# Block-diagonal 128x128 products in the chunk inverse of a gated DeltaNet, with a new order of the scan stage

## What is computed

```python
m_low = where(strict, einsum('cd,ed->ce', k * beta, k) * decay, 0)
t_inv = solve(eye + m_low, eye)          # lower triangular, 64x64
u = t_inv @ (v * beta);  w = t_inv @ (k * beta * exp(g))
a_intra = (q @ k.T) * decay
# scan over the 16 chunks
v_new = u - w @ state
o = (q * exp(g)) @ state + a_intra @ v_new
state = state * exp(g_last) + (k * exp(g_last - g)).T @ v_new
```

## Time and profile before

| | |
|---|---|
| median of three runs | 1391.61 us |
| profiled execution, its own time | 1390.32 us |
| its span | 1388.5 us |
| PE busy | 1371.7 us (99%) |
| DVE, ACT, POOL busy | 1027.0, 606.9, 177.9 us |
| instructions | 21991 |

### The profile page before, as it was taken

One profiled execution on the slowest core, in us unless ns is written; L12 is line 12 of the kernel. 1 busy time (PEld: TensorE's weight loads), 2 busy tenths in 40 slices (PEclk: granted clock), 3 DMA queues, 4 the chain that ended last, 5 costly groups with the idle time before them and its releaser, 6 DMA issues.

```text
span 1388.5 us, 21991 instructions
## 1 busy us (share of the span) xinstructions
PE 1371.7 (99%) x8400; PEld 1139.1 (82%) x8400; DVE 1027.0 (74%) x1890; ACT 606.9 (44%) x1306; POOL 177.9 (13%) x163
## 2 busy tenths in 40 slices
PE   9999999999999999999999999999999999999997
PEld 8788888787888888788888888888888888888885
DVE  6999976866888887645268796666665777777778
ACT  4655534422444443532113545545555544444540
POOL 4322332230000000236700000000000000000002
PEclk9999999999999999999999999999999999999998
DMA  6233245766344531245612153344435875555423
GB/s 216 91 113 115 111 163 182 243 221 179 94 107 117 135 103 51 77 166 177 239 55 91 69 189 130 143 167 167 167 133 212 295 239 181 165 159 178 128 69 121
DMA packets 123496, 206.83 MB, mean 149 GB/s; under 512 B 40864, under 2 KB 61568, under 8 KB 121088
## 3 DMA queue, kind: packets, MB, share of 16 engines
q1 hardware_dynamic: 113312, 183.93, 39.8%
q10 hardware_dynamic: 10080, 21.50, 4.1%
HBM read 142.92 MB, written 62.47 MB: 148 GB/s over the span
## 4 chain that ended last, share of the span: by engine, by line
PE 88%; DVE 6%; DMA 3%; SPq 2%; issue 1%; ACT 0%; POOL 0%; ACTq 0%; DVEq 0%; POOLq 0%
PE ps L2223 7%; PE ps L2603 6%; PE ps L2604 6%; PE ps L2602 6%; PE ps L2587 6%; PE ps L2585 6%; PE ps L2586 6%; PE ps L2171 5%; PE ps L2173 5%; PE ps L2172 5%; PE ps L2289 4%; PE ps L2109 4%; PE ps L2111 4%; PE ps L2110 4%; PE ps L2479 2%; PE ps L2483 2%
## 5 line engine op out<-in xcount | busy, mean ns | idle before, releaser
L2602 PE MATMUL ps<-thi,shi 128*128 128x512 f32 x416 | 161.8, 389 | 0.0
L2603 PE MATMUL ps<-tlow,shi 128*128 128x512 f32 x416 | 161.8, 389 | 0.0
L2604 PE MATMUL ps<-thi,slow 128*128 128x512 f32 x416 | 161.8, 389 | 0.0
L947 ACT ACTIVATE thi<-b 128x512 fp32r<-128x512 f32 x104 | 65.5, 630 | 111.8 <-PE ps L2604 111.2
L1993 DVE TENSOR_TENSOR tlow<-b,thi 128x512 fp32r<-128x512 f32 x104 | 71.8, 690 | 52.8 <-ACT thi L947 52.7
L937 POOL TENSOR_TENSOR zt<-zt,ln2gb 128x256 f32<-128x256 f32 x4 | 3.4, 852 | 691.5 <-ACT zt L1403 691.5
L2602 PEld LDWEIGHTS ps<-thi,shi 128*128 128x128 f32 x416 | 78.1, 188 | 16.4
L2603 PEld LDWEIGHTS ps<-tlow,shi 128*128 128x128 f32 x416 | 78.1, 188 | 16.2
L2604 PEld LDWEIGHTS ps<-thi,slow 128*128 128x128 f32 x416 | 78.1, 188 | 16.1
L1986 DVE TENSOR_TENSOR slow<-sraw,shi 128x512 fp32r<-128x512 f32 x104 | 71.4, 686 | 21.6 <-ACT shi L947 20.9
L947 ACT ACTIVATE shi<-sraw 128x512 fp32r<-128x512 f32 x104 | 65.0, 625 | 28.9 <-DMA zt<-xpark 16.3
(11 more groups left out here) (445 smaller groups left out, 3827.2 us busy)
## 6 DMA issues: line engine op xcount, KB each, us to landing
raw<-in_wblk SPq DMA_DIRECT2D x55, 512.0 KB, 4.1
sraw<-hpark SPq DMA_DIRECT2D x104, 256.0 KB, 2.7
hpark<-hq SPq DMA_DIRECT2D x16, 1024.0 KB, 4.9
b<-in_wblk SPq DMA_DIRECT2D x64, 256.0 KB, 3.6
wraw<-in_wblk SPq DMA_DIRECT2D x30, 512.0 KB, 3.8
hpark<-hq SPq DMA_DIRECT2D x16, 768.0 KB, 4.9
park<-cb ACTq DMA_DIRECT2D x34, 256.0 KB, 3.3
park<-cacc ACTq DMA_DIRECT2D x12, 512.0 KB, 3.2
```

The costliest lines, as they stand in the source:

```text
L947: cp = lambda o_, i_: act.activation(o_, i_, ACT.Copy)
L2602: mm(outp, shi[s][:, ts], thi[m][:, :], start=first, stop=False, skip_group_check=True)
L2603: mm(outp, shi[s][:, ts], tlow[m][:, :], start=False, stop=False, skip_group_check=True)
L2604: return mm(outp, slow[s][:, ts], thi[m][:, :], start=False, stop=final, skip_group_check=True)
```

## The change

mm_ (128x256) becomes mmd (128 x 4 heads x 128), which DVE writes in two halves, each chunk's 64x64 block on the diagonal of its head's 128x128; the rest is zero. a_y then issues one product for each head, 128x128 weights by 64 moving columns, in place of two 64x64 ones. DVE's a_r of level 5 no longer writes rinv, but the two diagonal blocks of a new rind, and waits for the products b_vn of the tile before, which read it. b_vn takes rind's 128x128 as weights and all 128 rows of xs, with 128 moving columns as before. Three memsets set the zeros once. a_u, a_ut and a_t1 keep their blocks. The lists of PE, DVE and ACT in a step get another order, FILLS gets 31 gaps in place of 28 and other numbers (384 in all, as before), and SP's load_ks moves ahead of load_dec. load_pair is written out in place, with the same instructions. The diff, cut to its core:

```diff
--- before.py
+++ after.py
 N_STEP, N_LAST = 7 * NP, 8
 N_STD = 3
 FILLS = [
-    [1, 0, 0, 4, 0, 0, 0, 0, 0, 11, 0, 5, 1, 0, 1, 0, 4, 0, 1, 0, 1, 0, 0, 5, 6, 1, 2, 0],
-    [0, 3, 5, 0, 6, 1, 1, 0, 0, 3, 0, 2, 2, 3, 0, 3, 0, 0, 0, 0, 0, 0, 1, 0, 0, 1, 8, 2],
-    [0, 0, 0, 0, 0, 3, 2, 2, 1, 0, 0, 0, 0, 0, 0, 0, 4, 0, 0, 13, 0, 0, 1, 0, 0, 9, 0, 0],
-    [0, 0, 0, 0, 0, 3, 2, 2, 1, 0, 0, 0, 0, 0, 0, 0, 4, 4, 0, 9, 0, 0, 2, 0, 4, 4, 0, 0],
-    [0, 0, 0, 0, 0, 2, 0, 4, 2, 0, 0, 0, 0, 0, 0, 0, 4, 5, 0, 8, 0, 1, 2, 0, 2, 5, 0, 0],
-    [0, 0, 0, 0, 0, 3, 2, 2, 1, 0, 0, 0, 0, 0, 0, 0, 4, 5, 0, 8, 0, 1, 2, 0, 0, 7, 0, 0],
-    [0, 0, 0, 0, 0, 3, 2, 2, 1, 0, 0, 0, 0, 0, 0, 0, 4, 5, 0, 8, 0, 0, 1, 0, 4, 5, 0, 0],
-    [0, 0, 0, 0, 0, 3, 2, 2, 1, 0, 0, 0, 0, 0, 0, 0, 4, 0, 0, 13, 0, 0, 1, 0, 4, 5, 0, 0],
-    [0, 0, 0, 0, 0, 2, 4, 0, 2, 0, 0, 0, 0, 0, 0, 0, 0, 0, 0, 19, 1, 3, 0, 0, 0, 2, 0, 0],
-    [0, 0, 0, 3, 0, 4, 0, 8, 2, 1, 2, 0, 0, 0, 0, 1, 0, 19, 0, 0, 0, 0, 7, 0, 0, 4, 0, 6],
+    [2, 5, 0, 0, 0, 0, 0, 0, 5, 4, 0, 0, 1, 5, 2, 0, 0, 0, 3, 0, 1, 0, 0, 0, 2, 7, 0, 3, 0, 2, 1],
+    [5, 0, 7, 0, 0, 3, 0, 3, 0, 0, 3, 2, 1, 0, 3, 0, 0, 3, 0, 0, 0, 0, 1, 0, 0, 3, 2, 0, 0, 0, 8],
+    [0, 2, 0, 0, 0, 4, 1, 1, 0, 0, 0, 1, 0, 0, 0, 1, 1, 6, 0, 3, 1, 1, 0, 0, 0, 4, 1, 0, 3, 0, 0],
+    [2, 2, 0, 1, 0, 5, 0, 0, 0, 1, 0, 2, 0, 0, 0, 0, 0, 5, 0, 2, 5, 0, 1, 0, 0, 4, 1, 0, 7, 0, 0],
+    [0, 0, 0, 1, 0, 5, 0, 1, 0, 0, 0, 2, 0, 0, 0, 0, 1, 9, 0, 1, 0, 2, 0, 0, 0, 4, 2, 0, 6, 0, 0],
+    [0, 0, 0, 1, 0, 5, 0, 1, 0, 0, 0, 2, 0, 0, 0, 0, 1, 4, 0, 2, 3, 0, 1, 0, 0, 5, 1, 0, 2, 0, 0],
+    [3, 2, 0, 1, 0, 4, 1, 1, 0, 0, 0, 2, 0, 0, 0, 0, 0, 10, 0, 1, 0, 0, 1, 0, 0, 5, 0, 0, 5, 0, 0],
+    [2, 0, 0, 1, 0, 4, 1, 1, 0, 0, 0, 2, 0, 0, 0, 1, 1, 8, 0, 1, 2, 0, 0, 0, 0, 5, 0, 0, 3, 0, 0],
+    [1, 3, 0, 1, 0, 3, 2, 0, 0, 0, 2, 0, 0, 0, 0, 0, 0, 6, 0, 6, 1, 0, 2, 1, 0, 5, 0, 1, 1, 0, 0],
+    [0, 3, 0, 2, 1, 1, 6, 0, 0, 7, 1, 3, 0, 0, 0, 2, 0, 9, 3, 0, 7, 0, 0, 3, 6, 0, 0, 0, 4, 0, 6],
 ]
...
+        rind = workb("rind", 512, [P, NH, P])
+        mmd = at("mmd", 96, [P, NH, P], extra=26496)
-        mm_, ml, *tb = [worka(name, 256, [P, NH, CH]) for name in ("mm", "ml", "tb0", "tb1")]
+        ml, *tb = [worka(name, 256, [P, NH, CH]) for name in ("ml", "tb0", "tb1")]
...
                     load_dv(t + 2)
+                load_ks(t + 1, (t + 1) % 2)
                 if t < NT - 2:
                     load_dec(t + 2)
                 load_qk(t + 1)
-                load_ks(t + 1, (t + 1) % 2)
...
                 if t is not None: b_vn(t, 0)
+                if s in BEHIND: split_hi(BEHIND[s])
                 if a is not None: a_t1(a, q)
+                if a is not None: a_eg(a)
                 if t is not None: b_exps(t, 0)
+                if t is not None: b_vn(t, 1)
+                if t is not None: b_osq(t)
                 if t is not None: b_pt(t, 0)
-                if a is not None: a_eg(a)
-                if t is not None: b_vn(t, 1)
-                if s in BEHIND: split_hi(BEHIND[s])
+                if first < last: late_half(first)
                 if t is not None: b_ya(t, 0)
-                if t is not None: b_osq(t)
-                if first < last: late_half(first)
+                if n is not None: a_scalars(n, p)
+                if n is not None: a_squares_k(n)
                 if t is not None: b_exps(t, 1)
-                if n is not None: a_scalars(n, p)
                 if n is not None: a_squares_q(n)
-                if n is not None: a_squares_k(n)
                 if t is not None: b_pt(t, 1)
+                if t is not None: b_ya(t, 1)
                 if first + 1 < last: late_half(first + 1)
                 if first + 2 < last: late_half(first + 2)
-                if t is not None: b_ya(t, 1)
...
+                dve.memset(mmd[:, :, :], 0.0)
+                dve.memset(rind[:, :, :], 0.0)
+                dve.memset(xs[CH:P, :, :], 0.0)
...
                 tt(ml[:, :, :], half(A0, 0), em0[:, :, :], ALU.mult).then_inc(m_ok, 1)
-                tt(mm_[:, :, :], half(A0, 0), eml[:, :, :], ALU.mult).then_inc(m_ok, 1)
+                for r in chunks:
+                    ins = tt(mmd[r, :, r], half(A0, 0)[r], eml[r, :, :], ALU.mult)
+                ins.then_inc(m_ok, 1)
                 dve.wait_ge(m_ok, 2 * t + 1)
                 tt(tb[0][:, :, :], bh(msk(M_ID)), ml[:, :, :], ALU.subtract).then_inc(t1_ok, 1)
 
                 dve.wait_ge(u_mm, 5 * t + l)
                 if l == 1:
                     dve.wait_ge(r0_ok, t + 1)
-                tt(rinv[p][:, :, :], rinv[p][:, :, :], half(A1, 0), ALU.subtract).then_inc(r_ok if l < 5 else a_done, 1)
+                if l < 5:
+                    tt(rinv[p][:, :, :], rinv[p][:, :, :], half(A1, 0), ALU.subtract).then_inc(r_ok, 1)
+                else:
+                    if t:
+                        dve.wait_ge(vn_mm, 2 * t)
+                    for r in chunks:
+                        ins = tt(rind[r, :, r], rinv[p][r, :, :], half(A1, 0)[r], ALU.subtract)
+                    ins.then_inc(a_done, 1)
...
                 if t is not None: b_max(t, 0, p)
+                if t is not None: b_state(t, 0, p)
                 if a is not None: a_att(a, q)
                 if s == -1: clear()
-                if t is not None: b_state(t, 0, p)
-                if t is not None: b_prob(t, 0)
                 if a is not None: a_ys(a, 1)
                 if t is not None: b_x(t, 1, p)
                 if a is not None: a_tb(a, 1)
                 if a is not None: a_r(a, 1, q)
+                if t is not None: b_prob(t, 0)
                 if a is not None: a_ys(a, 2)
-                if a is not None: a_qeg(a, q)
+                if s in BEHIND: split_lo(BEHIND[s])
                 if a is not None: a_tb(a, 2)
                 if a is not None: a_r(a, 2, q)
-                if s in BEHIND: split_lo(BEHIND[s])
+                if a is not None: a_qeg(a, q)
+                if t is not None: b_state(t, 1, p)
                 if a is not None: a_ys(a, 3)
+                if t is not None: b_on(t, p)
+                if a is not None: a_r(a, 3, q)
+                if a is not None: a_tb(a, 3)
                 if t is not None: b_max(t, 1, p)
-                if t is not None: b_on(t, p)
-                if a is not None: a_tb(a, 3)
-                if a is not None: a_r(a, 3, q)
-                if t is not None: b_state(t, 1, p)
                 if a is not None: a_ys(a, 4)
-                if t is not None: b_prob(t, 1)
+                if n is not None: a_kd(n, p)
                 if t is not None: b_yd(t)
                 if a is not None: a_r(a, 4, q)
                 if a is not None: a_tb(a, 4)
+                if t is not None: b_prob(t, 1)
+                if a is not None: a_ys(a, 5)
                 if n is not None: a_norm(n, p)
-                if a is not None: a_ys(a, 5)
-                if n is not None: a_kd(n, p)
+                if a is not None: a_r(a, 5, q)
                 if n is not None: a_ee(n)
                 if n is not None: a_vb(n, p)
-                if a is not None: a_r(a, 5, q)
...
                     pe.wait_ge(r_ok, 4 * t + (l - 1))
-                blocks(half(A0, 0), mm_, rinv[p]).then_inc(y_mm, 1)
+                for h in range(NH):
+                    last = mm(half(A0, 0)[:, h, :], mmd[:, h, :], rinv[p][:, h, :], start=True, stop=True)
+                last.then_inc(y_mm, 1)
...
             def b_vn(t, c, p):
-                r = slice(c * CH, (c + 1) * CH)
                 if c == 0:
                     pe.wait_ge(a_done, t + 1)
                     if t < NT - 1:
                         pe.wait_ge(vb_ok, t + 2)
                 pe.wait_ge(x_ok, 2 * t + (c + 1))
                 for h in range(NH):
-                    last = mm((C0h, C1h)[c][r, h, :], rinv[p][r, h, :], xs[r, h, :], start=True, stop=True)
+                    last = mm((C0h, C1h)[c][:, h, :], rind[:, h, :], xs[:, h, :], start=True, stop=True)
                 last.then_inc(vn_mm, 1)
...
                 fill(f[0])
                 if t is not None: b_ks(t, 0, p)
                 fill(f[1])
+                if a is not None: a_kq(a, q)
+                if a is not None: a_kk(a, q)
                 if t is not None: b_scores(t, 0)
                 fill(f[2])
-                if a is not None: a_kk(a, q)
+                if t is not None: b_vn(t, 0, p)
                 fill(f[3])
-                if a is not None: a_kq(a, q)
-                if t is not None: b_vn(t, 0, p)
+                if a is not None: a_t1(a)
                 fill(f[4])
-                if a is not None: a_t1(a)
+                if t is not None: b_ds(t, 0, p)
                 fill(f[5])
-                if t is not None: b_ds(t, 0, p)
+                if a is not None: a_y(a, 1, q)
                 fill(f[6])
-                if a is not None: a_y(a, 1, q)
+                if t is not None: b_ks(t, 1, p)
                 fill(f[7])
-                if t is not None: b_ks(t, 1, p)
```

(53 more changed lines are left out.)

## The result

The changed kernel takes 1409.2 us (median; 1407.7 to 1411.3) against 1391.8 of before: ratio 1.0131, 95% interval 1.0118 to 1.0143. Forecast were 1406 us and a range of 1399 to 1411. It is slower by 17.4 us.

A forecast was written before the change was run, and what follows sets the result against it. PE was taken as the bound, never stalling in the scan stage. Its work +13.7 us and one wait +1.0 make +14.7 on a span of 1388.5, 1403.2, so a median of 1406 us; range 1399 to 1411.

The forecast's parts named there:

- changes of kind: PE switching between products with 128x128, 128x64 and 64x64 weights, 0.14 to 0.20 each; 165 become 132, -5.1 us.
- Part 1: PE's 40 a_y groups: eight wide records each, paced by the weight load at 0.112 a record, +17.2 us.
- Parts 2 to 4: On PE: wide b_vn +0.4 us, fewer changes of kind -5.1 us, b_o's partly lost overlap +1.2 us.
- Part 4: b_o on PE keeps its overlap on one side and loses the other, 0.17 in each of seven steps, +1.2 us.
- C to B: PE going from products with 64x64 weights to products with 128x64 weights, 0.15 extra.
- C to A: PE going from 64x64 to 128x128 weights, 0.20 extra: the first group ends 0.10 later, the next product takes 0.33, not 0.23.
- Part 5: DVE, ACT, queues: added DVE half writes cost nothing; a_y 1 waits once for ACT's copy behind split_hi, +1.0 us.
- The signs that the prediction named: In the trace after: a_y records 0.11 apart, stage 286 us, b_vn 0.90, 1 us gap before step 3's a_y 1.
- That moving columns decide: Rival for wide a_y on PE: pace 0.058, so the 17.2 goes; 1389, not slower; chance 0.14.
- That DVE gets late: Rival: DVE's two added halves and a_norm behind level 5 are not covered, up to +4.8 more, 1411; chance 0.12.
- the work as summed: The main case: PE's work costs what the prices add up to, 1404 to 1408; chance 0.66.
- the second rival: DVE's added halves make PE wait for tb or xs in every step, up to +4.8 more, 1411; chance 0.12.

The follow-up runs named there:

- The moved fill: The kernel after with one fill of steps 0 to 6 moved from behind b_ds 0 to ahead of a_t1; 1407.8 us, stage 287.81.
- split_later: The kernel after with split_hi one place later in ACT's list, behind the copy that a_y of level 1 waits for; 1408.3 us, stage 287.63.

## Why the prediction was right

The sum of PE's own work, by the same prices, beside the measured stage:

| kernel | changes of kind | sum, us | stage, us | difference |
|---|---|---|---|---|
| before | 165 | 271.7 | 271.75 | 0.1 |
| old order, wide b_vn | 183 | 275.3 | 277.37 | 2.1 |
| old order, wide a_y | 127 | 285.3 | 288.23 | 2.9 |
| new order, narrow both | 216 | 282.0 | 284.88 | 2.9 |
| new order, wide b_vn | 210 | 281.4 | 284.32 | 2.9 |
| new order, wide a_y | 150 | 288.0 | 291.07 | 3.1 |
| after (both wide) | 132 | 285.4 | 288.67 | 3.3 |

(The expectations above have 281.9 for the fourth kernel; the prices as printed give 282.0.) In the new order the difference is 2.9 to 3.3 whatever the products are, but it is not made of the same waits. About 1.0 is a_y 1 behind the copy in step 3, and 0.67 the first branch product. The rest stands mostly at b_vn 1, which waits for xs, when both products are narrow (0.12 in five steps, 0.35 in one), and at b_vn 0 and a_t1 in the kernel after. In the old order the difference is 0.1 with the products of before and 2.1 and 2.9 with one of them wide: these waits come with DVE's halves, not with the order. (In the earlier trace rows the names ps<-tb,ys and ps<-ys,tb are a_ut and a_u, in the order of the list; the prices are the same for both.)

**Part 1, a_y.** Right: 0.11 a record, with 32, 64 or 128 moving columns. (The 0.107 fits the shortest loads of the earlier trace rows; the medians, 0.108 and 0.192 for 32 and 128 columns, give 0.112. With 0.107 a record the term would be 15.6, so it does not give the same 17.2.) The trace of after has all 320 of its loads at the length of every other 128-column load (duration ns, min/median/max):

```profile
L2311 PEld LDWEIGHTS ps<-rinv,mmd x320: 186/192/193, 325.1 to 567.0; 128*128 128x128 f32 x160
```

The Trainium skill, TensorE: Matmul & The Clock Gate, LDWEIGHTS, counts a load by its columns, and these runs agree: 0.107 of the 0.11. By the formula in its Back-to-back issue gap, which goes by moving columns alone, the three kernels with 32, 64 and 128 columns would differ widely; they don't. The same section keeps that formula for an isolated product, and says that in a stream of loads and products both set the spacing. That fits these runs: a fill with 512 columns takes 0.23, and a_y 0.11 a record with 32 to 128.

**Parts 2 to 4.** Right in sum: with both products narrow, the sum for the new order was 282.0 and for after 285.4; the measured step between them is 3.8, the sum's 3.4. That the changes of kind could give back only 5.1 of 17.6 was the core of the forecast. Part 4 can be read by itself: from b_o to b_ds, with a_ut and a_u between, after takes 2.06 where the prices alone give 2.44; that is 0.38 of overlap left of 0.53, so 0.15 lost a step for the 0.17 forecast. One reading was loose: the 431.06 to 431.68 of the earlier trace rows is 0.62, and b_pv behind it is B, so it prices C to B and not C to A. The price of 0.10 holds all the same: narrow a_y between fills takes 0.61 (433.57 to 434.18).

**Part 5.** The 1.0 us for the copy behind split_hi was right in place, step and size (0.90 in the list, 1.04 when taken away). The cost at nothing was wrong, for a_t1 and for b_vn 0. The slack at a_t1 by my numbers, 3.4 against 3.0 plus 0.33, was too small to cost at nothing, and two half writes cost 0.88 to the next start and not 0.67. From the start of b_scores to that of a_t1, the five steps 0, 2, 3, 5 and 6 take 0.26 to 0.34 more than the sum, and steps 1 and 4 nothing: 1.5 in all. The moved fill recovered 0.86. In steps 2, 3, 5 and 6 part of it is b_vn 0 behind xs, 0.08 to 0.16 each. The 7 or 8 fills that should have covered the writes of rind and a_vb did not do so in steps 2 and 3: there DVE works all but without a pause from the first half of rind (408.07 in step 2) to tb. Smaller waits of 0.1 to 0.25 stand at one b_vn 1 and one b_ds. The first branch product was 0.67 late, 0.5 of it waiting for ACT's yh; this I had not looked at. What puts ACT late there I didn't test.

**The size.** Forecast span 1403.2, measured 1407.9: 2.3 of the 4.7 missing are these waits in the stage, 1.1 lie behind it and 1.4 ahead, where the same code varies by as much from kernel to kernel. The signs that the prediction named came out mixed: 286 us was to be the stage, and the stretches around it were to keep their lengths. Of the 1.1 behind the stage 0.3 belongs to the new order: it is lost between the first four branch products in the kernel after, with both products narrow, with 128 columns and with the moved fill alike, and that whole part lasts 809.6 in all four kernels with the old order and 809.9 to 810.7 in the eight with the new one. The other 0.7 stands at L2616, where PE waits 0.5 for DVE's tlow; the split_later kernel, with the same products, doesn't show that wait, and whose it is stays open.

**The rivals.** That moving columns decide is refuted by the two column runs. That DVE gets late was right in kind: it happens at a_t1 and b_vn 0, for a third of the 4.8 I gave it, and behind level 5 too. The measured 1409.2 lies above the 1404 to 1408 given for the work as summed, between it and this rival's 1411: the main term was right, and a part of the second rival came on top.

## What to carry to other kernels

Price a matrix engine that is never idle by the distances between starts, in classes of rows and columns of the weights, and add a price for each change of class; that sum told seven kernels apart to within their waits. Here a product with 32 to 128 moving columns costs what its 128 weight columns cost, so putting two 64x64 blocks on a diagonal to use the whole array doubles its price in a run of its kind (0.47 to 0.90), and still loses where it stands alone among wide work (0.82 to 0.90). It pays only among wide work and for products that did not run in pairs before (b_vn: 2.4 us of the stage in the new order). Whether a wide or a narrow form is better can't be told from the product: ask which runs of equal shape it joins and which it cuts.

## What the runs showed that I had not expected

The order of the list alone costs 13.1 us with the products of before in it, wide a_y alone costs 16.5 in the old order, and both together with wide b_vn only 16.9: the two don't add, since the new order brings changes of kind and the wide products take them away again. Two DVE writes of 64 partitions in place of one of 128 took 0.88 to the next start in place of 0.33; each half lasts as long as the whole did (0.85 for the two, 0.41 for one), so half the partitions save nothing. And products of two disjoint quadrants, issued in turn instead of one quadrant after the other, took 1.02 in place of 1.51.
